# GDN recurrence: unread TensorE matmuls between the steps of the first chunk's preparation and in three of its slots

## The chip, the cores and the metric

The kernel runs on one core of one Trainium2 chip. The metric is the device time of that core in microseconds (us), the median of three runs; lower is better. In the rows below, TensorE is PE (matmuls) and PEld (weight loads), VectorE is DVE, ScalarE is ACT, GpSimd is POOL, SyncE is SP.

## The reference, cut to what matters

The whole program is a three-block network for 512 positions of width 1024. The change lies in the gated delta rule ("GDN") of the second block's first layer: 6 heads, keys and values of width 128, in chunks. Per chunk (the kernel's chunks are 128 positions, so there are four):

```
gam = cumsum(g);  decay = exp(gam_i - gam_j), i >= j
kk = k k^T
lower = I + strict(beta_i * kk * decay)
u, w = solve(lower, [v * beta, k * beta * exp(gam)])
qk = (q k^T) * decay
step over the chunks, state S:
    delta = u - w S
    o     = (q * exp(gam)) S + qk delta
    S     = exp(gam_last) * S + (k * exp(gam_last - gam))^T delta
```

The kernel brings the solve into the form of an inverse (tile TT, from a base of small solved blocks, doubled up in two levels) that is then multiplied with v*beta - (k*beta*exp(gam)) S.

## The kernel before, in words

The program is a series of regions. A region (L543) is a block in which every engine has its own instruction stream, ordered by semaphores; at its end all engines meet at a barrier. The function that changes is `recurrence_region` (L2303), which lies between the window attention and the output projection of that layer.

The six heads go in two groups g of three. PSUM has eight banks: group g uses banks 3g, 3g+1 and 3g+2 for the preparation and the inverse, and bank 6+g for the steps that touch the state. A chunk n is prepared by seven steps on TensorE, each for both groups:

- p1 (L2345): spreads gam over 128 partitions (three matmuls with 6 contraction rows; two tiny ones more for g = 0). DVE and ACT make decays and exp(gam) of it.
- p2 (L2356): the same for beta; it waits for ACT's read of p1's bank (`gl`).
- p3 (L2362): k k^T, after ACT has copied beta out of the bank (`bb`). DVE makes the matrix `mt` of it, for which POOL must have made `x` from decays and beta.
- p4 (L2369): k q^T, waits for `mt`. DVE makes `qk` of it.
- p5 (L2376): transposes k, waits for `qk`. ACT scales the rows out (`kr`, L2537).
- p6 (L2382): transposes v, waits for `kr`. ACT scales the rows out (`vr`, L2548).
- p7 (L2388): transposes TT, waits for `vr` and for `tt0` (DVE, `first_level`, L2687). DVE comes to `first_level` in its own order, after `keys` of both groups (L2711), and `keys` waits for `eb` from POOL (L2805).

Then each chunk n has seven slots. In a slot TensorE does, group by group, one step of the inverse of chunk n (slot 0: `a`, slot 1: `b`, slot 2: `turn_inverse`, slot 3: `a` again, slot 4: `b` again), one state step of chunk n-1 (s1 to s4, head_sums), and the preparation step p1 to p7 of chunk n+1. The order is written out by hand (L2470 to L2498). For n = 0 there is no chunk before, so no state step, and banks 6 and 7 are not used until slot 0 of n = 1, where s1 writes them.

Each engine takes its instructions in order: what is queued behind a TensorE matmul waits for it. The operands of this region are plain float32. A float32 matmul shows as two MATMUL records in the trace (three heads: x6), a float32 transpose as one.

The kernel has these few lines where the change goes in (L2466 to L2469):

```
            pe.wait_ge(keep["loaded"], 16 * 2)
            for prepare in (p1, p2, p3, p4, p5, p6, p7):
                for g in range(G):
                    prepare(0, g)
```

Of the kernel before, what the change touches and what calls it, by code (L numbers as in the profile page):

```python
# [139 lines left out]
class Weights:  # L140
# [36 lines left out]
    def chunk(self, A, name, n, part):  # L177
        depth = A[name].shape[2]
        k = 8 * part
        kc = min(8, depth - k)  # L180
        self.order[name, n, part] = len(self.source)
        self.source.append([A[name][n, :, k:k + kc, :]])
        self.after[name, n] = len(self.source)
        if part == 0:
            self.unit[name, n] = self.units
            self.units += 1
# [2116 lines left out]
def recurrence_region(nc, C, PS, E, QKVZ, BETA, GAM, O, keep):  # L2303


    H, G = GDN_HEADS, 2
# [18 lines left out]
    def at(n, g):  # L2325
        return G * n + g + 1
# [4 lines left out]
    with region(nc, "a_sums", "t_sums", "tt_sums", "spread", "betas", "kk", "kq", "k_turned", "v_turned", "t_turned",  # L2331
# [8 lines left out]
        def _(pe):  # L2340
            def each(g):
                a, b = heads[g]
                return [(h, slice((h - a) * P, (h - a + 1) * P)) for h in range(a, b)]
# [51 lines left out]
            def s1(n, g):  # L2395
                if n:
                    pe.wait_ge(R["sums_read"], at(n - 1, g))
                    pe.wait_ge(R["st"], at(n - 1, g))
                else:
                    pe.wait_ge(R["cleared"], 1)  # L2400
                pe.wait_ge(R["kb"], at(n, g))
                for h, o in each(g):
                    last = nc.tensor.matmul(PS[6 + g][:, o], QKVZ[:, H + h, chunk(n)], ST[:, h, :], start=True, stop=True)
                last.then_inc(R["s1"], 1)

            def s2(n, g):
                pe.wait_ge(R["r"], at(n, g))
                pe.wait_ge(R["tt_ready"], lv(n, LATE - 1, g))
                for h, o in each(g):
                    last = nc.tensor.matmul(PS[6 + g][:, o], TT[n % 2][:, h, :], R_[:, h, :], start=True, stop=True)  # L2410
                last.then_inc(R["s2"], 1)

            def s3(n, g):
                pe.wait_ge(R["u"], at(n, g))
                pe.wait_ge(R["qe"], at(n, g))
                pe.wait_ge(R["qk"], at(n, g))
                for h, o in each(g):
                    nc.tensor.matmul(PS[6 + g][:, o], ST[:, h, :], QKVZ[:, h, chunk(n)], start=True, stop=False)
                    last = nc.tensor.matmul(PS[6 + g][:, o], U[:, h, :], QK[n % 2][:, h, :], start=False, stop=True)
                last.then_inc(R["s3"], 1)  # L2420

            def s4(n, g):
                pe.wait_ge(R["o"], at(n, g))
                pe.wait_ge(R["kr"], at(n, g))
                for h, o in each(g):
                    last = nc.tensor.matmul(PS[6 + g][:, o], KR[n % 2][:, h, :], U[:, h, :], start=True, stop=True)
                last.then_inc(R["s4"], 1)

            def head_sums(n, g):
                if n + 1 < NT:  # L2430
                    pe.wait_ge(R["st"], at(n, g))
                else:
                    pe.wait_ge(R["o"], at(n, g))
                pe.wait_ge(R["o_sq"], at(n, g))
                a, b = heads[g]
                nc.tensor.matmul(PS[6 + g][:, 0:3 * P], C["mean_head"][:], R_[:, a:b, :].rearrange("p h t -> p (h t)"),
                                 start=True, stop=True).then_inc(R["head_sums"], 1)

            def a(n, late, g):
                if late:  # L2440
                    pe.wait_ge(R["t_ready"], at(n, g))
                    pe.wait_ge(R["masked_last"], at(n, g))
                else:
                    pe.wait_ge(R["t0"], at(n, g))
                    pe.wait_ge(R["masked"], at(n, g))
                    if n:
                        pe.wait_ge(R["w_ready"], lv(n - 1, LATE - 1, g))
                for h, o in each(g):
                    last = nc.tensor.matmul(PS[3 * g][:, o], BT[late][:, h, :], T[:, h, :], start=True, stop=True)
                last.then_inc(R["a_sums"], 1)  # L2450

            def b(n, late, g):
                pe.wait_ge(R["w_ready"], lv(n, late, g))
                if n or late:
                    pe.wait_ge(R["tt_ready"], lv(n, late, g) - G)
                for h, o in each(g):
                    last = nc.tensor.matmul(PS[3 * g + 2][:, o], W1[:, h, :], TT[n % 2][:, h, :], start=True, stop=True)
                last.then_inc(R["tt_sums"], 1)

            def turn_inverse(n, g):  # L2460
                pe.wait_ge(R["tt_ready"], lv(n, 0, g))
                for h, o in each(g):
                    last = nc.tensor.transpose(PS[3 * g][:, o], TT[n % 2][:, h, :], C["ident"][:])
                last.then_inc(R["t_sums"], 1)

            pe.wait_ge(keep["loaded"], 16 * 2)  # L2466
            for prepare in (p1, p2, p3, p4, p5, p6, p7):
                for g in range(G):
                    prepare(0, g)  # L2469
            for n in range(NT):  # L2470
                before, after = n - 1, n + 1
                for slot in range(7):
                    for g in range(G):
                        if slot == 0:
                            a(n, 0, g)
                        if slot == 1:
                            b(n, 0, g)
                        if slot == 2:
                            turn_inverse(n, g)
                        if slot == 3:  # L2480
                            a(n, 1, g)
                        if slot == 4:
                            b(n, 1, g)
                        if before >= 0:
                            if slot == 0:
                                s1(before, g)
                            if slot == 1:
                                s2(before, g)
                            if slot == 2:
                                s3(before, g)  # L2490
                            if slot == 3:
                                s4(before, g)
                            if slot == 5:
                                head_sums(before, g)
                        if after < NT:
                            (p1, p2, p3, p4, p5, p6, p7)[slot](after, g)
                        elif slot == 6:
                            s1(n, g)  # L2498
            for g in range(G):
                s2(NT - 1, g)  # L2500
            for g in range(G):
# [1555 lines left out]
```

## Time and profile before

| | us |
|---|---|
| Median of 3 runs | 2823.52 (2822.82 to 2828.8) |
| The profiled execution's own time | 2820.41 |
| Its span, first to last instruction | 2818.6 |
| PE busy | 2605.4 (92%) |
| DVE busy | 1464.8 (52%) |
| ACT busy | 1057.6 (38%) |
| POOL busy | 457.9 (16%) |

The span is the time between the first and the last instruction of the profiled execution; its own time is 1.8 us longer. Times in the rows are counted from the start of the span. The granted clock of TensorE is a share of 2.4 GHz: 1.00 is 2.4 GHz and 0.50 is 1.2 GHz. Over the whole span it is 0.957. Matmul records overlap, because matmuls are pipelined: what a matmul costs in a series is the distance from its start to the start of the next group, not its duration.

### The profile page before, as it was taken

Reading aid. Unit: us, or ns where it says so; the run is one execution under the profiler, and the core shown is the slowest. Engines: PE = TensorE matmul, PEld = TensorE weight load, DVE = VectorE, ACT = ScalarE, POOL = GpSimd, SP = SyncE. Lnnn points to the kernel's source line nnn. Section 1 sums busy time; section 2 is a strip of 40 time slices with the busy share of each in tenths; the row PEclk is TensorE's granted clock in tenths of the full one; section 3 lists DMA queues with packets and bytes.
Section 4 is the critical chain, followed back from the end, with each engine's and each line's share of the span. In section 5 each row is a group of like instructions: output and inputs, shape, how many; then the busy total and the mean of one; then the engine's idle time right before and its main releaser. Section 6 shows DMA issues by size and latency. Waiting matters only on the chain. (4 is left out here: it accounts for less than half of the span.)

```text
span 2818.6 us, 31986 instructions
## 1 busy us (share of the span) xinstructions
PE 2605.4 (92%) x12550; PEld 2070.7 (73%) x12550; DVE 1464.8 (52%) x2097; ACT 1057.6 (38%) x1598; POOL 457.9 (16%) x399
## 2 busy tenths in 40 slices
PE   8898898899899999978998888999998988899997
PEld 5676887677678888756787776877786856687775
DVE  5645554354456662265323555667534355676643
ACT  4653443433342322233414454222224355322223
POOL 4544443001010000000006323000020131200002
PEclk9999899899999999999998799999999999999999
DMA  6224001332023323221221002222332211122231
GB/s 209 100 96 136 1 1 68 112 108 98 23 90 100 102 89 95 86 68 63 79 82 39 1 31 66 91 90 90 106 96 94 92 36 38 55 93 92 90 109 56
DMA packets 89429, 223.64 MB, mean 79 GB/s; under 512 B 19897, under 2 KB 36553, under 8 KB 88091
## 3 DMA queue, kind: packets, MB, share of 16 engines
q1 hardware_dynamic: 84920, 207.11, 22.6%
q10 hardware_dynamic: 4360, 14.49, 1.4%
q8 instruction: 101, 1.65, 0.2%
q14 instruction: 48, 0.39, 0.0%
HBM read 214.41 MB, written 12.39 MB: 80 GB/s over the span
## 5 line engine op out<-in xcount | busy, mean ns | idle before, releaser
L235 DVE TENSOR_TENSOR w_low<-w_raw,w_high 128x1024 fp32r<-128x1024 f32 (+2 forms) x337 | 405.8, 1206 | 851.1 <-ACT w_high L225 850.9
L297 PE MATMUL bank<-x_high,w_high 128*128 128x512 f32 x1840 | 746.9, 406 | 32.1 <-DVE x_low L491 20.4
L298 PE MATMUL bank<-x_low,w_high 128*128 128x512 f32 x1840 | 733.2, 398 | 0.0
L299 PE MATMUL bank<-x_high,w_low 128*128 128x512 f32 x1840 | 730.3, 397 | 0.0
L225 ACT ACTIVATE w_high<-w_raw 128x1024 fp32r<-128x1024 f32 (+2 forms) x380 | 386.2, 1019 | 603.1 <-PE bank L299 502.0
L297 PEld LDWEIGHTS bank<-x_high,w_high 128*128 128x128 f32 x1840 | 349.5, 190 | 140.7 <-issue 52.8
L298 PEld LDWEIGHTS bank<-x_low,w_high 128*128 128x128 f32 x1840 | 349.6, 190 | 86.4 <-issue 5.5
L299 PEld LDWEIGHTS bank<-x_high,w_low 128*128 128x128 f32 x1840 | 348.9, 190 | 86.3
L297 PE MATMUL bank<-f_high,w_high 128*128 128x512 f32 x528 | 208.8, 395 | 0.9 <-DVE w_low L235 0.9
L299 PE MATMUL bank<-f_high,w_low 128*128 128x512 f32 x528 | 209.1, 396 | 0.0
L298 PE MATMUL bank<-f_low,w_high 128*128 128x512 f32 x528 | 209.1, 396 | 0.0
L235 POOL TENSOR_TENSOR w_low<-w_raw,w_high 128x1024 fp32r<-128x1024 f32 x43 | 105.2, 2448 | 141.1 <-ACT w_high L225 141.0
L297 PEld LDWEIGHTS bank<-f_high,w_high 128*128 128x128 f32 x528 | 99.1, 188 | 27.8 <-issue 3.1
L408 POOL TENSOR_TENSOR ln_half<-x 128x512 f32<-128x512 f32 x4 | 6.9, 1717 | 683.8 <-DVE x L3730 683.8
L298 PEld LDWEIGHTS bank<-f_low,w_high 128*128 128x128 f32 x528 | 99.1, 188 | 24.6 <-issue 0.5
L299 PEld LDWEIGHTS bank<-f_high,w_low 128*128 128x128 f32 x528 | 99.1, 188 | 23.2
L3643 ACT ACTIVATE f_high<-gate 128x512 fp32r<-128x512 f32 x44 | 27.8, 632 | 214.9 <-DVE gate L3761 214.9
L297 PE MATMUL bank<-o_high,w_high 128*128 128x512 f32 x192 | 78.4, 408 | 10.3 <-DVE o_low L560 10.3
L3640 ACT ACTIVATE gate<-gate 128x512 f32<-128x512 f32 x44 | 27.8, 632 | 155.0 <-DVE gate L722 155.0
L299 PE MATMUL bank<-o_high,w_low 128*128 128x512 f32 x192 | 77.4, 403 | 0.0
L298 PE MATMUL bank<-o_low,w_high 128*128 128x512 f32 x192 | 76.8, 400 | 0.0
L1027 DVE TENSOR_TENSOR raw<-bank,rstd 128x512 f32<-128x512 f32 x38 | 25.8, 686 | 96.6 <-PE bank L299 77.2
(621 smaller groups left out, 3935.2 us busy)
## 6 DMA issues: line engine op xcount, KB each, us to landing
w_raw<-in_ffn_in_dram SPq DMA_DIRECT2D x132, 512.0 KB, 3.2
w_raw<-in_ffn_out_dram SPq DMA_DIRECT2D x48, 512.0 KB, 3.5
w_raw<-in_gdn_in_dram SPq DMA_DIRECT2D x24, 512.0 KB, 3.2
w_raw<-in_mix_in_dram SPq DMA_DIRECT2D x22, 512.0 KB, 3.8
w_raw<-in_ffn_out_dram SPq DMA_DIRECT2D x24, 384.0 KB, 3.2
w_raw<-in_swa_qk_dram SPq DMA_DIRECT2D x12, 512.0 KB, 3.2
bias_rows<-bias_row ACTq DMA_DIRECT2D x4, 1280.0 KB, 14.3
w_raw<-in_mix_gate_a_dram SPq DMA_DIRECT2D x8, 512.0 KB, 3.2
```

Of the source, the lines that this page charges most:

```text
L225: self.nc.scalar.activation(self.high[c % SPLIT][:, 0:w], self.raw[c % RAW][:, 0:w], ACT.Copy).then_inc(self.high_done, 1)
L235: (on or self.nc.vector).tensor_tensor(self.low[c % SPLIT][:, 0:w], self.raw[c % RAW][:, 0:w], self.high[c % SPLIT][:, 0:w].bitcast(F32), ...
L297: nc.tensor.matmul(out, wh, high[:, k, :], start=first + at == 0, stop=False)
L298: nc.tensor.matmul(out, wh, low[:, k, :], start=False, stop=False)
L299: last = nc.tensor.matmul(out, wl, high[:, k, :], start=False, stop=first + at == depth - 1)
L408: self.nc.gpsimd.tensor_tensor(self.half[:], self.x[:, 0, :], self.x[:, 1, :], ALU.add).then_inc(self.S["half_ok"], 1)
L1027: W.freed(nc.vector.tensor_tensor(raw[i % 3][:], W.bank(PS, name, n)[:], rstd[:], ALU.mult), name, n)
L3640: nc.scalar.activation(g[i % 2][:], g[i % 2][:], ACT.Silu).then_inc(R["act_ready"], 1)
L3643: nc.scalar.activation(FH[:, i, :], g[i % 2][:], ACT.Copy).then_inc(R["f_high"], 1)
```

## The change

A helper `filler(times)` is added that multiplies the 128x128 identity with a 128x512 slice of the GDN input (`QKVZ[:, 3 * H, :]`, float32) into the whole of bank 7. Nothing reads the result and no semaphore is raised by it or waited for. It is issued four times at the start of TensorE's stream in this region, three times behind each preparation step of chunk 0 (six times behind p6), and twice behind each of slots 1, 2 and 4 of chunk 0: 4 + 6 x 3 + 6 + 3 x 2 = 34 matmuls.

```
@@ -2463,10 +2463,17 @@
+            def filler(times):
+
+                for _ in range(times):
+                    nc.tensor.matmul(PS[7][:], C["ident"][:], QKVZ[:, 3 * H, :], start=True, stop=True)
+
+            filler(4)
             pe.wait_ge(keep["loaded"], 16 * 2)
             for prepare in (p1, p2, p3, p4, p5, p6, p7):
                 for g in range(G):
                     prepare(0, g)
+                filler(6 if prepare is p6 else 3)
             for n in range(NT):
                 before, after = n - 1, n + 1
                 for slot in range(7):
@@ -2496,6 +2503,8 @@
                             (p1, p2, p3, p4, p5, p6, p7)[slot](after, g)
                         elif slot == 6:
                             s1(n, g)
+                    if before < 0 and slot in (1, 2, 4):
+                        filler(2)
             for g in range(G):
                 s2(NT - 1, g)
```

## Rows read from the trace of the kernel before

**Rows 1.** The page, busy time, share of the span and instructions of each engine
```profile
PE 2605.4 (92%) x12550; PEld 2070.7 (73%) x12550; DVE 1464.8 (52%) x2097; ACT 1057.6 (38%) x1598; POOL 457.9 (16%) x399
```

**Rows 2.** Busy time by stretch; columns: length, PE, PEld, DVE, ACT, POOL, PEclk, DMA, GB/s
```profile
1543.00:1546.40 3.40, 2.25 (x19) 1.88 (x18) 0.29 (x1) 0.66 (x1) 0.00 (x0) 1.00 0.74 116
...
1547.80:1563.40 15.60, 14.30 (x60) 12.72 (x61) 6.28 (x17) 4.31 (x15) 5.65 (x6) 0.50 0.00 1
1563.50:1566.80 3.30, 0.85 (x6) 0.38 (x4) 1.27 (x1) 2.01 (x8) 3.30 (x4) 1.00 0.00 0
...
1568.30:1583.00 14.70, 14.68 (x58) 12.80 (x58) 3.52 (x12) 3.46 (x9) 0.00 (x0) 0.50 0.01 1
1583.00:1587.30 4.30, 4.30 (x21) 4.26 (x21) 1.58 (x3) 2.37 (x7) 1.30 (x2) 0.50 0.00 0
1587.40:1595.10 7.70, 6.42 (x52) 5.52 (x52) 6.08 (x10) 4.68 (x15) 5.82 (x6) 1.00 0.00 0
1595.10:1619.60 24.50, 23.71 (x191) 21.70 (x189) 15.29 (x34) 13.51 (x38) 9.51 (x10) 1.00 0.00 1
```

**Rows 3.** Timeline of PE, preparation of chunk 0 (start, length, line, count, idle before)
```profile
1547.84 1.62 PE L2349 MATMUL bank<-gam,pick 6*128 6x128 f32 x6 [2.13 <-PEq L551]
...
1551.93 2.92 PE L2359 MATMUL bank<-beta,pick 6*128 6x128 f32 x12 [0.34 <-ACT gl L2514]
...
1558.56 2.93 PE L2372 MATMUL bank<-qkvz 128*128 128x128 f32 x12 [0.85 <-DVE mt L2677]
...
1568.32 1.51 PE L2392 MATMUL bank<-ident,tt 128*128 128x128 f32 x6 [3.76 <-DVE tt L2687]
```

**Rows 4.** Timeline of ACT, POOL and DVE, 1563.8 to 1568.7
```profile
1563.85 1.67 ACT L2548 ACTIVATE v_rows<-bank,col 128x128 f32<-128x128 f32 x6
...
1566.06 0.99 POOL L2805 TENSOR_TENSOR exp_gam<-exp_gam,beta 128x384 f32<-128x384 f32 x1
...
1567.62 1.02 DVE L2687 TENSOR_TENSOR tt<-edge_solved,level_mask 128x384 f32<-128x384 f32 x2
```

**Rows 5.** Timeline of PE, plain float32 matmuls of 512 columns, at 1.2 and 2.4 GHz
```profile
2410.20 2.05 PE L442 MATMUL bank<-ln_squares,over_d 128*128 128x512 f32 x2 [0.19 <-POOL ln_squares L429]
2412.04 1.70 PE L444 MATMUL bank<-x,over_d 128*128 128x512 f32 x2
...
2800.06 1.02 PE L442 MATMUL bank<-ln_squares,over_d 128*128 128x512 f32 x2
2800.92 1.07 PE L444 MATMUL bank<-x,over_d 128*128 128x512 f32 x2
```

**Rows 6.** Timeline of PE, chunk 0's end and chunk 1, at 2.4 GHz
```profile
1595.23 0.83 PE L2449 MATMUL bank<-t,bt 128*128 128x128 f32 x6
...
1596.67 0.93 PE L2349 MATMUL bank<-gam,pick 6*128 6x128 f32 x6
...
1597.87 0.94 PE L2449 MATMUL bank<-t,bt 128*128 128x128 f32 x6
...
1601.80 0.93 PE L2359 MATMUL bank<-beta,pick 6*128 6x128 f32 x6
1602.66 0.94 PE L2457 MATMUL bank<-tt,w 128*128 128x128 f32 x6
1603.43 0.83 PE L2410 MATMUL bank<-rhs,tt 128*128 128x128 f32 x6
...
1613.81 0.83 PE L2457 MATMUL bank<-tt,w 128*128 128x128 f32 x6
1614.48 0.49 PE L2379 MATMUL bank<-ident,qkvz 128*128 128x128 f32 x3
1614.81 0.83 PE L2457 MATMUL bank<-tt,w 128*128 128x128 f32 x6
```

**Rows 7.** Timeline of PE, 512-column matmuls of a projection, split operands, at 2.4 GHz
```profile
1705.06 0.39 PE L297 MATMUL bank<-o_high,w_high 128*128 128x512 f32 x1
1705.29 0.39 PE L298 MATMUL bank<-o_low,w_high 128*128 128x512 f32 x1
```

More of the change, by code:

```diff
@@ L2464, in turn_inverse, with filler @@
                 last.then_inc(R["t_sums"], 1)
+            def filler(times):
+                for _ in range(times):
+                    nc.tensor.matmul(PS[7][:], C["ident"][:], QKVZ[:, 3 * H, :], start=True, stop=True)
+            filler(4)
             pe.wait_ge(keep["loaded"], 16 * 2)
@@ L2469, in _ @@
                     prepare(0, g)
+                filler(6 if prepare is p6 else 3)
             for n in range(NT):
@@ L2498, in _ @@
                             s1(n, g)
+                    if before < 0 and slot in (1, 2, 4):
+                        filler(2)
             for g in range(G):
```

## The prediction

> **What bounds the kernel now.** I read four views in this order. The page first: PE is busy for 92% of the span and no other engine for more than 52% [rows 1], so whatever is added to TensorE's stream costs its full length unless it falls into a stretch in which TensorE waits. Then the busy time by stretch around the changed region, because the added matmuls compute nothing that is used: all they can do is fill TensorE's time and so act on its granted clock. The reader is to see the clock column there [rows 2]. TensorE stands at 1.00 (2.4 GHz) until 1546.4, while it is busy for 2.25 of 3.40 us. It is at 0.50 (1.2 GHz) from the region's first matmul at 1547.84 to about 1563.4, at 1.00 for one stretch of 3.3 us in which it has almost nothing to do, and at 0.50 again until 1587.3. From 1587.4 it is at 1.00 for the rest of chunk 0 and for chunk 1. So chunk 0 is prepared, and the first half of its inverse made, at half clock. Third, the timeline of PE shows where it waits in the preparation: 0.34 us before p2, 0.85 before p4, and 3.76 before p7 [rows 3]. The last is no wait for TensorE's own results of that moment: ACT had the v rows at about 1565.5, but POOL finished `eb` of the second group at 1567.05, DVE then did `keys` for it and came to `first_level` at 1567.62, and p7 started at 1568.32 as soon as the first half of that pair was there [rows 4]. Fourth, the price of the steps at 2.4 GHz is in chunk 1 [rows 6].
>
> The stretch that the change can touch ends where chunk 1's first `a` starts, at 1595.23 [rows 6]. From 1547.84 that is **47.4 us**. Behind it PE is busy for 23.71 of 24.50 us at full clock [rows 2], the order of the work is unchanged, and the next regions start behind a barrier: a shift at 1595.23 goes through to the end of the program one for one.
>
> **What one filler costs.** It is a plain float32 matmul, 128x128 with 512 moving columns. The layer norm issues the same shape back to back: starts at 2800.06 and 2800.92, at 2.4 GHz [rows 5]; the distance is 0.86 us and I take **0.855 us** (two records of 0.43). At 1.2 GHz the pair at 2410.20 lasts 2.05 us with its run-out and the next starts 1.84 us later [rows 5]; twice the fast price is **1.71 us** and I take that. The 34 fillers are then 29.1 us of TensorE at 2.4 GHz. That is more than half of the 47.4 us, and TensorE's waits in there are 5 us in all [rows 3], so the question is whether the clock gives back the difference.
>
> **The part ahead of p1.** Before the change p1 starts as soon as the barrier opens, so the four fillers lie on the path with their full length. Bounds: 3.4 us if the clock never falls, 6.8 us if all four run at 1.2 GHz. Between them: before the rise at 1563.4 TensorE did 128-row matmuls from 1558.56 on with hardly a gap (4.9 us) [rows 2, 3], and before the rise at 1587.4 it did nothing else than such ones from 1583.0 on (4.3 us) [rows 2]. I take 4.9 us at low clock, which is 2.87 fillers, and 1.13 at high clock (0.97 us): **5.9 us**.
>
> Here the Trainium skill has a rule (TensorE: Matmul & The Clock Gate, section "Why this matters for your kernels"): keep TensorE busy for 4 us continuously and the clock comes up. By that rule the four would take 4.0 + 1.66 x 0.855 = 5.4 us, half a microsecond less. The trace does not bear the rule out as it stands: from 1568.30 to 1583.00 PE is busy for 14.68 of 14.70 us at 0.50 throughout [rows 2]. What lay in that stretch were the 6-row matmuls of p1 and p2 between 128-row ones, so what TensorE does seems to count, not only that it is busy.
>
> **The work itself, at 2.4 GHz.** The distances of chunk 1 [rows 6]: six records with 128 rows 0.67 us (1613.81 to 1614.48), 0.77 behind a 6-row group (1602.66 to 1603.43), six 6-row records 0.86 (1601.80 to 1602.66), p1 of the first group with its two small matmuls 1.20 (1596.67 to 1597.87), three transposes 0.33 (1614.48 to 1614.81).
> - p1 to p6: 2.06 + 1.72 + 1.34 + 1.34 + 0.66 + 0.66 = 7.8 us; p7: 0.7 us.
> - Slots 0 to 4 of chunk 0: 0.67 + 1.20 + 0.77 + 0.86 = 3.5; 2 x (0.77 + 0.86) = 3.3; 2 x (0.33 + 0.67) = 2.0; 4 x 0.67 = 2.7; 2 x (0.67 + 0.33) = 2.0; together 13.5 us.
> - Behind the filler of slot 4: p6 0.7, then ACT's v rows of two groups (half of 1.67 each [rows 4], 1.6) and the last transposes of p7, 0.3: 2.6 us, to chunk 1.
>
> **The fillers behind the steps.** 24 between the steps and 6 in the slots, 30 x 0.855 = **25.7 us**. What they cover: the wait ahead of p4 is a chain from p2's end (1551.93 + 2.92 = 1554.85) to 1558.56, 3.7 us [rows 3]; two sets of fillers (5.1) and p3 (1.3) are longer, so p4 no longer waits. The wait ahead of p7 is a chain from p4's end (1561.49) to 1568.32, 6.8 us [rows 3, 4]; p5, p6 and twelve fillers are 1.3 + 10.3 = 11.6 us. So of these twelve 4.8 us cover nothing even with all of the wait subtracted, and p7's start is set by TensorE. The shorter waits of p2, p5 and p6 (under 2 us each with a 2.6 us filler set ahead) go the same way. In chunk 0, mt of chunk 1 gates p4 3.7 us behind p2; slots 2 and part of 3 with their fillers are 6.1 us. In slot 5 ACT's k rows (about 1.8 us) are covered by the two fillers of slot 4 (1.7). Nothing new is waited for, no semaphore moves, and no queue but TensorE's has anything added. DMA costs nothing here: its share is 0.00 to 0.01 from 1547.8 on [rows 2].
>
> **The sum.** 5.9 + 7.8 + 0.7 + 13.5 + 25.7 + 2.6 = **56.2 us** against 47.4: **8.8 us slower**. Put as gain and loss: without the fillers the same work at full clock would be 24.6 us and its waits; the fillers take 5.9 + 25.7 = 31.6. Against the profiled execution's own time, 2820.41 + 8.8 = 2829.2. The median of the runs shown is 3.1 us above that execution, so I forecast a median of **2832 us**. A measurement of this kernel tells about 0.2% (5.6 us) from no change.
>
> **The rivals.**
> - *The clock doesn't fall at the region's start.* It fell only about 1.4 us before p1, behind work of PE at 2.25 of 3.40 us [rows 2]. If the fillers come in time to hold it, the four cost 3.4 instead of 5.9 us: +6.3 us, 2829.8 as a median and 2826.7 on the profiled execution's level. For it: the fall is close. Against: nothing in the change comes before the barrier. 8%.
> - *The clock falls again among p1 and p2.* Their 6-row matmuls are what stood in the long low stretch [rows 2]. Against it, chunk 1 has both kinds mixed and stays at 1.00 [rows 2, 6]. If p1, p2 and their two sets of fillers ran low, 2.06 + 1.72 + 5.1 = 8.9 us are added: +17.7, 2841. If it stays low through all of the preparation, 8.5 + 20.5 = 29 us are added: 2861. 13% together, nearly all on the first, and less where only a part of it is low. The Trainium skill's other rule (same page and section) is that only idle gaps over about 3 us bring the clock down; by it this rival is empty, since no such gap is left. The trace shows a fall at 1546.4 without such a gap before it.
> - *Faster: a filler costs less than the layer norm's row says.* The projections' 512-column matmuls, on split operands, start 0.23 us apart [rows 7]. At that price the sum, again first part, preparation, chunk 0: 1.9 (all four at low clock) + p1 2.1 + a set 0.7 + p2 1.7 + the 3.7 us chain that then binds again + p4 1.3 + the 6.8 us chain + p7 0.7 + a set 0.7 + slots 13.5 + six fillers 1.4 + 2.6 = 37.1 us, 10.3 less than now: 2813. The point from which it decides: by my sum, 24.6 us of work and 37 filler prices (the four ahead count for about seven), the total is 47.4 at 0.62 us per filler; faster below, slower above. Against: the fillers' operands are plain float32, and the rows of that kind are at 0.86 [rows 5]. 4%.
> - *The change does nothing* (the unread matmuls are dropped on the way to the chip, or the clock gives back exactly what they take): 2823 to 2824. 3%.
>
> **How the numbers follow.** The forecast case, clock up within the first fillers and held, has 72%. Its own bounds are the first part (-2.5, +0.9 us), the chance position of the clock's later falls in the rest of the program, and the spread of the runs shown (6 us from lowest to highest): 2828 to 2836. The range reaches to the first rival below (2826) and into the second above (2840). Slower by over 0.2% takes most of the forecast case, the second rival and part of the first: 0.83. Within 0.2%: 0.12, of which the forecast case gives 0.06 by spread. Faster: 0.05.
>
> **What the profile would show.** Right: 68 MATMUL records of identity and qkvz at 128x512, 0.43 us apart; clock at 1.00 from about 1553 on through the region; no wait of PE ahead of p7; p7 at about 1580 instead of 1568; slots 0 to 4 in some 14 us plus 5 for fillers; chunk 1's first `a` at about 1604; everything behind it shifted by 9 us. Wrong: fillers under 0.62 us each, a clock row at 0.50 between 1554 and 1600, or p7 still waiting for DVE.

## The result, and the profile after

The changed kernel takes **2837.26 us** (median of five runs, 2833.74 to 2840.32) against 2823.48 before (five runs, 2819.12 to 2828.8): ratio 1.005, 95% interval 1.0039 to 1.0061, 13.8 us slower. The profiled execution took 2837.26 us with a span of 2835.4, which is 16.8 us more than the span before.

The page's head, which answers to [rows 1]:

```profile
span 2835.4 us, 32122 instructions
...
PE 2624.9 (93%) x12618; PEld 2074.5 (73%) x12618; DVE 1464.4 (52%) x2097; ACT 1057.5 (37%) x1598; POOL 458.0 (16%) x399
```

There are 68 more PE records, the two of each of the 34 fillers, and PEld has as many more. DVE, ACT and POOL have as many instructions as before.

The timeline of PE in the changed kernel, from the start of the region to chunk 1's first `a`. L2469 is the filler; columns as in [rows 3].

```profile
1547.88 6.17 PE L2469 MATMUL bank<-qkvz,ident 128*128 128x512 f32 x8 [3.10 <-PEq L551]
1553.98 0.93 PE L2349 MATMUL bank<-gam,pick 6*128 6x128 f32 x6
...
1566.86 1.50 PE L2372 MATMUL bank<-qkvz 128*128 128x128 f32 x12
1568.19 2.74 PE L2469 MATMUL bank<-qkvz,ident 128*128 128x512 f32 x6
1570.77 0.82 PE L2379 MATMUL bank<-ident,qkvz 128*128 128x128 f32 x6
...
1579.81 0.82 PE L2392 MATMUL bank<-ident,tt 128*128 128x128 f32 x6
...
1583.04 0.83 PE L2449 MATMUL bank<-t,bt 128*128 128x128 f32 x6
...
1586.73 1.38 PE L2457 MATMUL bank<-tt,w 128*128 128x128 f32 x6
...
1592.77 3.78 PE L2469 MATMUL bank<-qkvz,ident 128*128 128x512 f32 x4
1596.35 0.85 PE L2463 MATMUL bank<-ident,tt 128*128 128x128 f32 x3
...
1606.91 0.82 PE L2385 MATMUL bank<-ident,qkvz 128*128 128x128 f32 x6
1608.38 0.55 PE L2392 MATMUL bank<-ident,tt 128*128 128x128 f32 x3 [0.65 <-ACT v_rows L2557]
1609.15 0.55 PE L2392 MATMUL bank<-ident,tt 128*128 128x128 f32 x3 [0.23 <-ACT v_rows L2557]
1609.54 0.93 PE L2449 MATMUL bank<-t,bt 128*128 128x128 f32 x6
```

Three things are to be seen. The waits before p2, p4 and p7 of [rows 3] are gone: between the first filler at 1547.88 and the transposes at 1608.38 nothing stands in brackets, in the rows left out here as well. A set of three fillers takes 2.58 us (1568.19 to 1570.77), so 0.86 each. And p7 starts at 1579.81 where it started at 1568.32. The stretch from the region's first matmul to chunk 1's first `a` is 61.7 us instead of 47.4.

The same kernel by stretch, columns as in [rows 2]:

```profile
1547.80:1552.90 5.10, 5.02 (x6) 2.19 (x7) 0.00 (x0) 0.00 (x0) 0.74 (x1) 0.50 0.10 17
1553.00:1579.80 26.80, 26.80 (x109) 15.31 (x108) 8.50 (x21) 6.42 (x22) 8.62 (x8) 1.00 0.00 0
1579.80:1587.00 7.20, 7.20 (x43) 5.38 (x42) 1.28 (x7) 2.06 (x6) 0.00 (x0) 1.00 0.01 2
1587.10:1597.30 10.20, 10.20 (x33) 7.13 (x32) 2.36 (x6) 2.75 (x10) 0.99 (x1) 0.50 0.00 0
1597.40:1609.50 12.10, 11.22 (x77) 8.75 (x75) 8.01 (x12) 5.61 (x17) 7.28 (x7) 1.00 0.00 1
```

The clock comes up within the first fillers and is held through the preparation. Then it falls to 0.50 at 1587.1, in slots 0 and 1 of chunk 0, though TensorE had been busy for all of the 7.2 us before, and it stays there for 10.2 us.

**Where the 16.8 us are.** 14.3 are in this stretch (61.7 against 47.4). From chunk 1's first `a` to the start behind the last wait for `rhs` the kernels take 67.9 and 67.8 us. 1.7 us are at the region's tail. In both profiles the clock falls there for a short time, but over other work. In the kernel before it is low from 1662.5 to 1665.9, over the twelve matmuls ahead of the wait for `delta`, and that wait ends 4.7 us behind their start in both kernels. In the changed one it is low from 1682.6 to 1686.0, over the matmuls behind that wait. The changed kernel's timeline of PE there:

```profile
1682.18 0.49 PE L2418 MATMUL bank<-qkvz,state 128*128 128x128 f32 x2 [3.12 <-ACT delta L2586]
...
1683.67 0.64 PE L2418 MATMUL bank<-qkvz,state 128*128 128x128 f32 x2
1684.10 0.63 PE L2419 MATMUL bank<-qk,delta 128*128 128x128 f32 x2
```

and of the kernel before:

```profile
1668.50 0.39 PE L2419 MATMUL bank<-qk,delta 128*128 128x128 f32 x2
1668.72 0.39 PE L2418 MATMUL bank<-qkvz,state 128*128 128x128 f32 x2
```

The pairs are 0.43 us apart there and 0.22 before. From the start behind the last wait for `rhs` to the next region's first projection it is 14.8 us against 13.1. The last 0.7 us lie behind that, in regions that are the same in both kernels (1143.2 us against 1142.5). All fourteen profiles of this study show one or the other there: 13.1 to 13.2 (before, e4, e7, e8, e11, e12) or 14.6 to 15.3 (the rest). e5 and e12 are the same kernel and show 14.8 and 13.1, so it is part of the spread between executions. The difference of the medians, 13.8 us, is near the stretch's 14.3.

### The profile page after: what moved, and what is told of

Its sections match the earlier page's. It is cut to its first block and busy times, and to the rows that moved or that the text cites. A ratio compares the mean times of both kernels' runs of the same rounds, so it can differ in the third digit from the quotient of the medians.

```text
span 2835.4 us, 32122 instructions
## 1 busy us (share of the span) xinstructions
PE 2624.9 (93%) x12618; PEld 2074.5 (73%) x12618; DVE 1464.4 (52%) x2097; ACT 1057.5 (37%) x1598; POOL 458.0 (16%) x399
```

## The experiments

All lengths called "stretch" below run from the region's first matmul to chunk 1's first `a` in the one profiled execution of each kernel. "Theory K" is that matmuls with 6 contraction rows don't hold the clock, however busy TensorE is with them; "theory B" is that TensorE's busy time alone counts. "Theory M" adds to K that whether the clock falls in slots 0 and 1 hangs on where the moments at which it can change lie in the mix of 6-row and 128-row matmuls. The others are stated with the runs.

| kernel | stretch, us | clock falls in slots 0, 1 | median, us (runs) |
|---|---|---|---|
| before | 47.4 | already low | 2823.48 (5) |
| changed | 61.7 | yes | 2837.26 (5) |
| e1, changed again | 61.8 | yes | 2838.19 (1) |
| e2, fillers of 6 rows | 101.7 | already low | 2880.04 (1) |
| e3, changed, 128 rows in p1, p2 of chunk 1 | 55.9 | no | 2831.16 (1) |
| e4, before, the same edit | 43.4 | low until 1577.9 | 2817.82 (1) |
| e5, preparation's fillers alone | 53.4 | no | 2831.96 (10) |
| e6, slots' fillers alone | 51.8 | already low | 2832.21 (10) |
| e7, four fillers behind p6 alone | 40.7 | no | 2818.27 (12) |
| e8, e7 and four in slots 0, 1 | 43.3 | no | 2820.00 (12) |
| e9, changed, five at the start | 57.9 | no | 2838.26 (4) |
| e10, changed, none at the start | 54.0 | no | 2833.00 (8) |
| e11, e7 again | 43.7 | yes | 2821.95 (1) |
| e12, e5 again | 57.3 | yes | 2835.55 (1) |

**e1: the changed kernel once more.** No edit.

> The changed kernel once more, for a second profile. The first profile shows the granted clock at 0.50 from 1546.1 to 1552.9 and again from 1587.1 to 1597.4, in slots 1 and 2 of chunk 0. Theory K (6-row matmuls do not hold the clock, however busy TensorE is with them): the second fall is a fixture, it comes again within a few us of slot 1 (1584 to 1591) and lasts until 128-row work has run for a while; chunk 1 starts at 1608 to 1611. Theory P (chance: the fall belongs to that one execution): no fall between 1554 and 1605, and chunk 1 starts at about 1604 as the sum of the prediction said.

The stretch is 61.8 us, and the busy time by stretch, clock third from the end:

```profile
1554.00:1587.90 33.90, 33.90 (x151) 20.62 (x150) 9.79 (x28) 8.50 (x28) 8.61 (x8) 1.00 0.00 0
1588.00:1598.20 10.20, 10.20 (x33) 7.13 (x32) 2.34 (x6) 2.84 (x10) 0.99 (x1) 0.50 0.00 0
```

The same fall, at the same place in the code, for the same 10.2 us. It was not the chance of one execution, or not only (see e12).

**e2: the same fillers with 6 rows.**

```
-nc.tensor.matmul(PS[7][:], C["ident"][:], QKVZ[:, 3 * H, :], start=True, stop=True)
+nc.tensor.matmul(PS[7][:], pick[:, 0, :], GAM[:, :], start=True, stop=True)
...
-            filler(4)
             pe.wait_ge(keep["loaded"], 16 * 2)
+            filler(4)
```

> The same 34 fillers with 6 contraction rows in place of 128 (same number of columns, so the same length at a given clock). The four at the start go behind the wait for the masks, where nothing is waited for. Theory K: the clock stays at 0.50 through all of the preparation and until 128-row work dominates in slots 2 and 3; 30 or more fillers run at 1.71 us, the first p7 starts at about 1547.8 + 6.8 + 15.6 + 36 = 1606 and chunk 1 at about 1640; span 30 us or more above the changed kernel. Theory B (TensorE's busy time alone counts, not the rows): the clock rises within 7 us of the first filler and the times are those of the changed kernel, chunk 1 at about 1609.

By stretch:

```profile
1549.40:1608.20 58.80, 58.75 (x115) 29.29 (x115) 8.33 (x21) 6.42 (x22) 9.00 (x9) 0.50 0.00 0
1608.20:1643.40 35.20, 35.20 (x109) 24.59 (x109) 5.88 (x16) 6.43 (x17) 3.94 (x4) 0.50 0.00 0
1643.60:1650.00 6.40, 5.75 (x38) 4.10 (x36) 5.51 (x8) 3.49 (x12) 3.85 (x4) 1.00 0.00 0
```

TensorE is busy for 58.75 of 58.80 us, and the clock doesn't rise in all that time. p7 starts 58.7 us behind the first filler (expected 58.2). It rises at 1643.5, in slot 3, whose own matmuls all have 128 rows. Busy time alone doesn't bring the clock up; theory B is out. What differs from the changed kernel is the fillers' operands, in their rows and in their values; the steps of the recurrence are the same. Chunk 1 came 11 us later than I expected (1651, not 1640), because the slots ran low as well, with their 6-row fillers.

**e3 and e4: 128-row operands in p1 and p2 of chunk 1.** The twelve matmuls that spread gam and beta of chunk 1 in slots 0 and 1 get other operands of the same width; the results are not gam and beta. In ACT the exponentials of that chunk are taken with scale 0, so that they stay finite. Chunks 1 to 3 thus compute other values with the same instructions.

```
+one, two = (C["mean_head"][:], C["mean_head"][:]) if n == 1 else (pick[:, h, :], GAM[:, chunk(n)])
-last = nc.tensor.matmul(PS[3 * g + 1][:, o], pick[:, h, :], GAM[:, chunk(n)], start=True, stop=True)
+last = nc.tensor.matmul(PS[3 * g + 1][:, o], one, two, start=True, stop=True)
```

and the same with BETA in p2.

> The changed kernel with the p1 and p2 matmuls for chunk 1 (12 in slots 0 and 1 of chunk 0) given 128-row operands of the same width; their results are not gam and beta of chunk 1, so chunks 1 to 3 compute other values in the same instructions. Theory K: the fall at 1587 goes away, the clock is at 1.00 from about 1553 to the end of the region, slots 1 and 2 with their fillers take 7 us instead of 12, chunk 1 starts at about 1604 (5 to 5.6 us earlier than in the changed kernel). Theory B or P: the clock in slots 1 and 2 is as in the repeat of the changed kernel.

The whole of chunk 0 behind the preparation is at full clock now (columns as before):

```profile
1583.60:1604.10 20.50, 19.63 (x137) 15.99 (x135) 11.65 (x24) 9.63 (x29) 8.28 (x8) 1.00 0.00 1
```

The stretch is 55.9 us, 5.8 less than in the changed kernel. The prediction's sum, made for a clock that holds, was 56.2. About 1.1 us of the 5.8 are not the clock: at 2.4 GHz a 128-row group takes a little less than a 6-row one, and slots 0 and 1 take 6.1 us in e3 and 7.2 in e9 below, where the clock is at 1.00 with the 6-row operands. One profile without a fall is weak evidence by itself, since e5, e9 and e10 below keep the 6-row operands and have none either. What makes it stronger is said with e11 and e12.

> The same two edits of operands on the kernel before. There the clock was at 0.50 from 1566.9 to 1587.3 with TensorE busy for all but the first 1.4 us. Theory K: with 128-row operands in slots 0 and 1 it rises within 3.5 to 8 us of p7's start at 1568.3, that is by 1572 to 1577; chunk 1 starts 4 to 7 us earlier than at 1595.2, by 1589 to 1591. Theory B: no change, the rise stays near 1587 and chunk 1 at 1595.

On the kernel before, by stretch:

```profile
1569.20:1577.80 8.60, 8.58 (x37) 8.01 (x38) 1.82 (x9) 2.41 (x6) 0.00 (x0) 0.50 0.00 0
1578.00:1592.10 14.10, 11.74 (x94) 10.29 (x93) 9.13 (x17) 7.98 (x25) 7.28 (x7) 1.00 0.00 1
```

p7 starts at 1569.2 here, and the clock is up 8.7 us later instead of 19 us later [rows 2]. The rise is 0.7 us later than the latest that I had expected. The stretch is 4.0 us shorter, 43.4. With e2 this carries theory K in both directions: exchange rows for fewer and the clock stays down, exchange them for more and it comes up earlier, at the same number of instructions. The low stretch of 20.5 us behind 1566.9 is in e6's profile too, and e4 has one of 10.2 us in its place; the distance from the clock's rise before it to chunk 0's first `a` is 6.3 to 6.5 us in all three. The transposes of p7, which also stand in that stretch, are the same in all three. Each exchange changes the operands' values along with their rows (`pick` is zeros and ones, `mean_head` 1/128 throughout), and no run separates the two. The changed kernel's own fillers, which have the identity as one operand and so are mostly zeros there, do bring the clock up. That speaks against the values and does not settle it.

**e5 and e6: one half of the fillers each.** e5 leaves out the `filler(2)` of the slots; e6 leaves out the four at the start and all of the preparation's.

> The changed kernel without the six fillers in slots 1, 2 and 4 of chunk 0. Length from the region's first matmul to chunk 1's first a (before: 47.4 us, changed: 61.7). Theory K with FIFO cost: the fall in slots 0 and 1 comes as before; the two fillers behind slot 1 (3.6 us, mostly at low clock), behind slot 2 (1.7) and behind slot 4 (1.7, partly hidden behind ACT's rows) go, slot 2 runs at low clock for it: 56 to 58 us. Rival (the slot fillers pay for themselves by bringing the clock up): 61 us or more.

> The kernel before with only the six fillers in slots 1, 2 and 4. The two behind slot 1 fall into the low stretch (3.4 us), the others into the high one (1.7 + 1.7, of which about 1 is hidden behind ACT's k rows): the stretch is 47.4 + 4 to 6 = 51 to 53 us, the rise stays near 1587 to 1591. Rival (128-row fillers bring the rise forward and give the time back): 47 us or less.

Medians: 2831.96 (ratio 1.0033, 1.0021 to 1.0044) and 2832.21 (1.003, 1.002 to 1.0041), so either half alone is slower than before and the two are not told apart. In e6 the stretch is 51.8, as expected: the first two fillers take 3.6 us in the low stretch and the rise stays where it was. Its median is 9 us above that of before while the stretch is only 4.4 longer. In its profile, the shortest of the ten runs, the span is 7.6 us longer than that of before: 4.4 in the stretch, 1.7 at the tail, about 1 ahead of the region and the rest behind it; what it is in the other nine runs is not shown. e5's stretch of 53.4 us is under what I had expected (56 to 58), for the clock did not fall in slots 0 and 1:

```profile
1583.70:1602.60 18.90, 16.54 (x125) 14.38 (x124) 10.77 (x24) 9.40 (x29) 7.30 (x7) 1.00 0.00 1
```

So the fall is no fixture of this code, and "the changed kernel's slot fillers cause it" became a possible reading. e12 was made for that.

**e7 and e8: fillers only where TensorE waits.** e7 is the kernel before with

```
             for prepare in (p1, p2, p3, p4, p5, p6, p7):
                 for g in range(G):
                     prepare(0, g)
+                if prepare is p6:
+                    filler(4)
```

and e8 has one `filler(1)` more behind each group's work in slots 0 and 1.

> The kernel before with only four fillers, behind p6, where TensorE waits for DVE for 3.76 us anyway. Theory K: they are free (3.4 us at 2.4 GHz), the clock that has just risen at 1563.5 is held over the wait, p7 and slot 0 run at 2.4 GHz (about 4 us instead of 8), it falls again in slot 0 or 1 for the 6-row matmuls; stretch 42 to 45 us, median 3 to 5 us below the kernel before. Rival (fillers always cost their length): 50 us. Rival (clock already low when they start, so 6.8 us long): 50 us as well, with p7 late by 3 us.

> As the one with four fillers behind p6, and one filler more behind each group's work in slots 0 and 1 of chunk 0 (four, 3.4 us at 2.4 GHz). Theory K: mixed in so, the 128-row work holds the clock through slots 0 and 1; what that saves (about 3 us in slot 1, 1.5 in slot 2) is what they cost: stretch within 1.5 us of the one with four fillers alone. If the clock falls all the same: 3 to 5 us more than with four.

The timeline of PE in e7, around p7:

```profile
1567.03 1.46 PE L2385 MATMUL bank<-ident,qkvz 128*128 128x128 f32 x6
1568.33 3.60 PE L2469 MATMUL bank<-qkvz,ident 128*128 128x512 f32 x8
1572.25 0.99 PE L2392 MATMUL bank<-ident,tt 128*128 128x128 f32 x6 [0.32 <-DVE tt L2694]
```

and its clock from there to chunk 1:

```profile
1567.90:1592.40 24.50, 21.66 (x141) 16.88 (x142) 13.51 (x28) 12.04 (x37) 10.38 (x10) 1.00 0.00 1
```

The four fillers fit into the wait for DVE with 0.32 us to spare: p7 starts 20.5 us behind the region's first matmul with them and did so without them (1547.84 to 1568.32, [rows 3]). The clock, up since 1567.7, is held over the wait and did not fall again in this execution. The stretch is 40.7 us, 6.7 less than before. The median is **2818.27 us, ratio 0.9979 (0.997 to 0.9989)**: faster than both kernels, by 4.8 us against the 2823.10 of the 35 runs of before beside it. e8 is at 0.9986 (0.9976 to 0.9996), which is not told apart from e7, with a stretch 2.6 us longer than e7's, so four more fillers cost most of their 3.4 us when the clock is high without them. Its clock held:

```profile
1569.30:1596.60 27.30, 24.84 (x150) 18.24 (x150) 13.61 (x28) 12.33 (x38) 10.60 (x11) 1.00 0.00 1
```

**e9 and e10: five and none at the start.**

> The changed kernel with five fillers at the start in place of four: one more, 0.86 us of TensorE. Plain cost: stretch from the region's first matmul to chunk 1's first a 61.8 + 0.9 = 62.7 us, median 0.9 above the changed kernel. Theory M (whether the clock falls in slots 0 and 1 hangs on where the moments at which it can change lie in the mix of 6-row and 128-row matmuls; in the two profiles of the changed kernel they lay badly, in the profile with the preparation's fillers alone well): the code is moved by one filler against those moments, the fall is gone in the profile, stretch about 56.9 us, and the median is 3 to 5 us below the changed kernel though one more matmul is run.

> The changed kernel without the four fillers at the start. p1 and the first set run at low clock (3.7 + 5.1 us in place of 2.1 + 2.6), the first part's 6.1 us go: stretch 1.9 us shorter with the same rest, that is 59.9 with a fall in slots 0 and 1 and 54.1 without. Rival: the first four are what brings the clock up, without them it stays low into p3 or p4: 62 us or more.

e9's profile fits theory M, one matmul more and a stretch 3.8 us shorter than the changed kernel's, 57.9:

```profile
1558.90:1611.40 52.50, 51.63 (x259) 33.87 (x258) 20.14 (x45) 17.02 (x53) 16.98 (x16) 1.00 0.00 0
```

The median does not: theory M had it 3 to 5 us below the changed kernel's, and 2838.26 (four runs, 2835.37 to 2846.05; ratio 1.006, 1.004 to 1.0081) is no lower. That half of the expectation failed: the fall was absent in the profiled execution, and nothing shows that one more filler moves it away in general. e10 has 54.0 us, the expected case without a fall (54.1), and a median of 2833.00, 1.0038 (1.0027 to 1.0048), against 1.005 of the changed kernel. Its rival, that the first four are what brings the clock up, is out: the preparation's own sets did it.

**e11 and e12: second profiles of e7 and e5.** No edits.

> A second profile of the kernel with four fillers behind p6 alone (first profile: stretch 40.7 us, no fall of the clock in chunk 0). Where the clock is high over the wait and stays so: 40 to 41 us. Where it falls in slots 0 and 1: 43 to 46. Both are under the 47.4 of the kernel before.

> A second profile of the kernel with the preparation's fillers alone (first profile: 53.4 us, no fall in slots 0 and 1). Theory M: the moments may lie otherwise in this execution; the stretch is either 53 to 54 (no fall) or 56 to 58 (fall), and the start of the low stretch against the region's first matmul says which. Rival (the fall in the changed kernel is caused by its slot fillers): never a fall here, 53 to 54.

Both show the fall that their first profiles did not. e11 and, below it, e12, by stretch:

```profile
1568.50:1578.50 10.00, 9.38 (x51) 6.21 (x50) 4.23 (x11) 4.18 (x14) 3.38 (x4) 1.00 0.00 0
1578.70:1588.70 10.00, 10.00 (x44) 9.10 (x44) 3.10 (x7) 3.41 (x10) 1.86 (x2) 0.50 0.01 2
```

```profile
1558.00:1592.00 34.00, 34.00 (x152) 20.71 (x151) 9.91 (x28) 8.64 (x28) 8.62 (x8) 1.00 0.00 0
1592.20:1602.20 10.00, 10.00 (x43) 9.10 (x43) 3.14 (x7) 3.42 (x10) 1.74 (x2) 0.50 0.00 0
```

The stretches are 43.7 and 57.3, against 40.7 and 53.4 of the same kernels without the fall. The fall costs 3.0 us in e11. Of the 4.0 us between e12 and e5, 1.0 lies ahead of p1, where the clock rose later in e12, and 3.0 are the fall. e12 has no filler in the slots, so the slot fillers don't cause it. Of eight profiles in which real 6-row matmuls of slots 0 and 1 are reached at full clock without fillers between them (the changed kernel twice, e5, e12, e7, e11, e9, e10), four show it, always for about 10 us. For kernels that share the whole preparation the distance from the clock's rise to chunk 0's first `a` goes with it: 30.1, 30.0 and 30.0 us in the three profiles with a fall (changed, e1, e12), 30.8 in both without (e5, e9). With four fillers behind p6 it is 5.9 us with the fall (e11) and 5.6 without (e7).

Two runs have the distance at which the clock fell, and other work in slots 0 and 1. In e3 it is 29.9 us, and with 128-row operands the clock held, where it fell at 30.0 to 30.1. In e8 it is 5.9 us as in e11, and with a 128-row filler behind each group's work it held, though these fillers also shift the work behind them; e8's stretch, 43.3, is then no longer than e11's 43.7, so there the four fillers paid for themselves. These two pairs are the better evidence for theory K in slots 0 and 1, since the difference in the distance is nearly out of them.

That the distance counts is what theory M says, and it would explain why the medians of e5 and e9 do not repeat what their profiles show, since that distance differs from one execution to the next. It is a pattern found afterwards in a few profiles, not a test: no run sets the moment by itself, and that is left open.

## Why the prediction was right, step by step

The direction and the range held: slower, 2837.26 within 2826 to 2840. So did the main mechanism: the fillers cost their length, and the clock gives back less. But the forecast case, "clock up within the first fillers and held", did not come as written. Its own bounds were 2828 to 2836, and one of the signs that the prediction had named as wrong is there, a clock row at 0.50 between 1554 and 1600. The measured median lies in the part of the range that was added for the second rival, whose price for a fall was 17.7 us where 4.8 came. That the range held is partly luck. The size was 13.8 us where 8.8 was forecast.

- **The price of a filler.** Taken as 0.855 us at 2.4 GHz from the layer norm's matmul; measured 0.86. The cheap-filler rival is out, and so is the one that the change does nothing.
- **The part ahead of p1.** Forecast 5.9 us, measured 6.1 (1547.88 to 1553.98). The clock was low from 1546.1 to 1552.9, so the first rival, that it doesn't fall there, did not come. In e5, where the clock rose 3.5 us behind the first filler in place of 5.0, it was 5.3.
- **The preparation.** p1 to p7 with 21 fillers: 7.8 + 18.0 = 25.7 us forecast, 25.8 measured (1553.98 to 1579.81). All waits are covered, p7 included. It is now set by TensorE, 11.5 us later than before.
- **What the twelve fillers around p5 and p6 cover.** The chain to p7 was put at 6.8 us, and the twelve fillers with p5 and p6 at 11.6, so 4.8 us of them covered nothing by the prediction's own count. e7 shows the size that fits: four behind p6, with 0.32 us left.
- **Slots 0 to 4.** Forecast 13.5 us of work and 5.1 of fillers at full clock from p7's set on; this is the term that failed. From chunk 0's first `a` at 1583.04 to the end of slot 4's fillers at 1606.91 it took 23.9 us, where the forecast has 18.6. In e9, without the fall, it took 19.1. So the fall is 4.8 us of the excess and 0.5 are the distances being a little longer than taken. The remaining 0.2 us are the part ahead of p1.
- **The end of the chunk.** Forecast 2.6 us, measured 2.6 (1606.91 to 1609.54).

The step that was mis-sized is "the clock up within the first fillers and held". The second rival had the mechanism right, that the 6-row matmuls let the clock fall, but I put it among p1 and p2 of chunk 0, where the change has fillers around them, and there, once up, it held in every profile. It fell where the change has none between the groups, in slots 0 and 1, at p1 and p2 of chunk 1. I held chunk 1 against the rival, since it mixes both kinds and stays at 1.00; but in chunk 0 the state steps are missing from those slots, so 4 groups of 8 are 6-row ones there, against 4 of 12 in chunk 1. That was to be read from the code. The prediction also laid the long low stretch of the kernel before to p1 and p2 without saying that p7's transposes stand in it; e4 shows that exchanging p1 and p2 alone halves it, 10.2 us in place of 20.5. Where the fall is absent the sum holds: 55.9 us in e3, and 57.9 less the fifth filler's 0.9 in e9, against 56.2. With the fall the changed kernel's stretch is 61.7, 5.5 us over the sum, and the median is 5.3 us over the forecast.

The weighing of the Trainium skill's rule (TensorE: Matmul & The Clock Gate, "Why this matters for your kernels") came out on the side of the rows. The rule, busy for 4 us continuously and the clock is up, fails in e2: 58.75 of 58.80 us busy at 0.50. Its other rule, that the clock stays up as long as no idle gap is over some 3 us, fails in the changed kernel: the fall at 1587.1 comes behind 7.20 us of which 7.20 were busy.

For the change itself: it does what it means to do in the preparation, and loses all the same. Held clock halves the work there, from about 15 to 8 us, but that work stood in chains over DVE, ACT and POOL that take the same time at any clock, so p7 could not have come more than a few us earlier; that is an estimate, for no run has the preparation at 2.4 GHz without fillers. 24 fillers at 0.86 us and four at more cannot be paid from that.

## What to carry to other kernels

A matmul issued to hold the clock costs its full length in this kernel unless TensorE would have waited there: find the wait in the timeline, and put in only as many as fit. Here four fit behind p6, and they alone make the kernel 0.2% faster, where all 34 make it 0.5% slower. Before trusting the clock to hold, look at which matmuls stand in the stretch and not at TensorE's busy share: in slots 0 and 1, where half of the groups have 6 contraction rows, it fell under full load in four profiles of eight.

## What the runs showed of the hardware that was not expected

- TensorE busy for 58.75 of 58.80 us, most of them 6-row matmuls, at 1.2 GHz throughout (e2). With 128-row operands in twelve matmuls of slots 0 and 1 the clock holds at 2.4 GHz (e3) or comes up 8.7 us behind p7 (e4).
- The same kernel, run again, differs by 3.0 us by whether the clock falls in one place (e7 and e11, e5 and e12), and by some 1.6 us by where the clock is low at the region's tail. The start of the region alone lies between 1547.8 and 1555.7 us over the profiles, though nothing ahead of it was changed. They are part of the 7 to 13 us that the runs of one kernel are apart, lowest to highest.
